# The linear half of the first expert bias: from TensorE to a row added by GpSimd

## The reference, cut to what matters

```python
def expert_block(args):
    xblk, e = args                                    # 128 tokens of expert e
    hh = xblk @ w1[e] + b1[e]                         # 1024 -> 2048, b1 is the "first bias"
    glu = jnp.minimum(hh[:, :D_FF], SWIGLU_LIMIT)     # first half of the 2048
    lin = jnp.clip(hh[:, D_FF:], -SWIGLU_LIMIT, SWIGLU_LIMIT)   # "linear" half
    act = glu * jax.nn.sigmoid(SWIGLU_ALPHA * glu) * (lin + 1.0)
    return act @ w2[e] + b2[e]
```

## Time and profile before

| | us | |
|---|---|---|
| median of three runs | 2273.63 | |
| profiled execution, whole | 2272.34 | |
| its span, first to last instruction | 2270.5 | 1.84 us lie around it |
| TensorE busy | 2235.7 | 98% |
| VectorE busy | 1768.0 | 78% |
| ScalarE busy | 1238.4 | 55% |
| GpSimd busy | 450.8 | 20% |

### The profile page before, as it was taken

The page is one execution under the profiler, slowest core; times in us unless marked ns, Lnnn a source line. Parts: engine busy times, 40 slices in busy tenths (PEclk is TensorE's granted clock), DMA queues, the critical chain, the costliest instruction groups (busy, mean ns, idle before and its releaser), DMA issues.

```text
span 2270.5 us, 30667 instructions
## 1 busy us (share of the span) xinstructions
PE 2235.7 (98%) x10681; PEld 1828.9 (81%) x10681; DVE 1768.0 (78%) x1652; ACT 1238.4 (55%) x1154; POOL 450.8 (20%) x422
## 2 busy tenths in 40 slices
PE   7999999999999999999999999999999999999997
PEld 3888888888887887888788888888888888888886
DVE  6756655555656766757899999999999999999996
ACT  6322132222225624632777777777777777777774
POOL 3000000000221131102522222232222222223222
PEclk9999999999999999999999999999999999999999
DMA  8322323131321121146899999999999999999995
GB/s 301 121 93 93 99 87 130 57 131 57 106 96 38 38 75 38 57 149 216 317 359 370 372 371 379 382 369 369 382 363 379 365 366 381 375 369 380 378 368 192
DMA packets 135517, 542.98 MB, mean 239 GB/s; under 512 B 16132, under 2 KB 24468, under 8 KB 101391
## 3 DMA queue, kind: packets, MB, share of 16 engines
q1 hardware_dynamic: 123192, 516.30, 60.2%
q0 software_dynamic: 11952, 21.44, 4.0%
q10 hardware_dynamic: 296, 4.21, 0.5%
HBM read 533.79 MB, written 26.38 MB: 247 GB/s over the span
## 4 chain that ended last, share of the span: by engine, by line
PE 95%; DMA 2%; DVE 1%; POOL 1%; issue 1%; ACT 0%; POOLq 0%; SPq 0%; DVEq 0%
PE ps L2263 90%; PE ps L2819 1%; PE ps L2831 1%; PE ps L2610 1%; DMA ar<-h_d,ar 1%; POOL list_d L865 1%; DMA ar<-in_ctx 0%; PE ps L2555 0%; DMA out_x<-ar,cur 0%; DMA raw<-in_w_mod 0%; PE ps L2501 0%; PE ps L2375 0%; DVE nmx L1866 0%; ACT hhi L1017 0%; PE ps L2708 0%
## 5 line engine op out<-in xcount | busy, mean ns | idle before, releaser
L2263 PE MATMUL ps<-whi,yhi 128*128 128x512 f32 x1072 | 346.4, 393 | 0.1
L2263 PE MATMUL ps<-hhi,yhi 128*128 128x512 f32 x1072 | 342.5, 389 | 0.0
L2083 DVE TENSOR_TENSOR hlo<-raw,hhi 128x2048 fp32r<-128x2048 f32 x132 | 302.7, 2294 | 47.2 <-ACT hhi L1324 47.2
L1324 ACT ACTIVATE whi<-raw 128x2048 fp32r<-128x2048 f32 x132 | 253.4, 1920 | 98.9 <-PE ps L2263 98.9
L2083 DVE TENSOR_TENSOR wlo<-raw,whi 128x2048 fp32r<-128x2048 f32 x132 | 298.8, 2284 | 3.3 <-ACT whi L1324 1.9
L1324 ACT ACTIVATE hhi<-raw 128x2048 fp32r<-128x2048 f32 x132 | 253.1, 1918 | 76.5 <-PE ps L2263 76.4
L1441 DVE TENSOR_TENSOR wlo<-raw,whi 128x2048 fp32r<-128x2048 f32 x56 | 128.2, 2289 | 159.4 <-ACT whi L986 159.4
L2263 PEld LDWEIGHTS ps<-whi,yhi 128*128 128x128 f32 x1072 | 201.2, 188 | 53.9 <-issue 12.1
L2263 PEld LDWEIGHTS ps<-hhi,yhi 128*128 128x128 f32 x1072 | 201.2, 188 | 41.8
L2263 PE MATMUL ps<-whi,hhi 128*128 128x512 f32 x592 | 233.3, 394 | 0.0
L2263 PE MATMUL ps<-whi,hlo 128*128 128x512 f32 x592 | 230.8, 390 | 0.0
(11 more groups left out here) (355 smaller groups left out, 4457.3 us busy)
## 6 DMA issues: line engine op xcount, KB each, us to landing
raw<-in_exp_w SPq DMA_DIRECT2D x264, 1024.0 KB, 8.3
ar<-in_exp_w SPq DMA_DIRECT2D x132, 1024.0 KB
raw<-in_w_in SPq DMA_DIRECT2D x44, 1024.0 KB, 5.1
raw<-in_w_mod SPq DMA_DIRECT2D x22, 1024.0 KB, 6.2
raw<-in_w_br_ret SPq DMA_DIRECT2D x8, 1024.0 KB, 5.3
ar<-in_x SPq DMA_DIRECT2D x8, 512.0 KB, 7.8
raw<-in_w_br_diff SPq DMA_DIRECT2D x4, 1024.0 KB, 5.2
raw<-in_w_out SPq DMA_DIRECT2D x4, 1024.0 KB, 10.7
```

Source lines behind the costliest of these rows:

```text
L1324: act.activation(e_whi[j % ESPL], e_raw[s], ACT.Copy).then_inc(e_hi, 1)
L2083: V.tensor_tensor(e_wlo[j % ESPL], e_raw[s], e_whi[j % ESPL].bitcast(F32), ALU.subtract).then_inc(e_lo, 1)
L2263: return pe.matmul(out, lhsT, rhs, start=start, stop=stop, skip_group_check=skip)
```

## The change

Banks 4 and 5 no longer get their bias from TensorE. `add_bias` keeps two matmuls (banks 2 and 3), and the first product of `up` now opens banks 4 and 5. The bias row of the linear half (with its 1) is stored once in a DRAM scratch by ScalarE's queue, and for every item SyncE's queue loads that item's row, broadcast to 128 partitions (512 KB), into `F(A_LIN)`. When `up(i)` is done, ScalarE copies banks 4 and 5 to `F(A_AC)` (`linear_out`), GpSimd adds the row in place (`add_linear_bias`, 128x1024), and VectorE clamps in place from SBUF and then multiplies. ScalarE's order becomes chunk 11, `linear_out`, `x_high`, `glu`; VectorE's becomes chunk 11, `x_low`, clamp, gate product. On GpSimd the addition stands between the selector and `next_gather`.

```diff
+            def load_linear_bias(e, i):
+                if not isinstance(i, int):
+                    sp.wait_ge(moe_step, i * 3)
+                sp.dma_start(F(A_LIN, D), acc_d[one(e), :].broadcast_to((P, D))).then_inc(b_loaded, 16)
...
+            sp.wait_ge(stored, 16 * (LT + 2))
+            load_linear_bias(0, 0)
             with sp.Fori(1, N_EXPERTS) as i:
                 for j in range(FIRST):
                     load_w1(i, i, j)
+                load_linear_bias(i, i)
                 for k in range(MOE_N - FIRST):
                     load_w2(i - 1, i, FIRST + k, k)
...
+            def add_linear_bias(i):
+                pool.wait_ge(b_loaded, i * 16 + 16 * (BIASES + 1))
+                pool.wait_ge(moe_step, i * 3 + 1)
+                hold()
+                pool.tensor_tensor(out=F(A_AC, D), in0=F(A_AC, D), in1=F(A_LIN, D), op=ALU.add).then_inc(moe_step, 1)
...
                 next_sel(i, e1)
+                add_linear_bias(i)
                 next_gather(i, code2, i * 4 + 1)
...
             next_sel(0, 1)
+            add_linear_bias(0)
             next_gather(0, 2, 1)
...
+            def linear_out(i):
+                act.wait_ge(e_used, chunk(i, FIRST - 1) + 1)
+                act.activation(F(A_AC, D), psf[:, 4 * COL:6 * COL], ACT.Copy).then_inc(moe_step, 1)
...
                 for j in range(ESPL, MOE_N - 1):
                     hi_e(i, j)
+                hi_e(i, MOE_N - 1)
+                linear_out(i)
+                x_high(i + 1)
                 glu(i)
-                hi_e(i, MOE_N - 1)
-                x_high(i + 1)
...
-            act.activation(bsrc[64:128, :], bsrc[64:128, :], ACT.Identity, bias=ones[64:128, 0:1]).then_inc(bias_hi, 1)
+            linear = F(A_LSRC, COL)[0:2 * N_EXPERTS, :]
+            act.activation(linear, linear, ACT.Identity, bias=ones[0:2 * N_EXPERTS, 0:1]).then_inc(bias_hi, 1)
+            act.activation(bias, F(A_BSRC, COL), ACT.Copy).then_inc(bias_hi, 1)
             act.wait_ge(bias_hi, 1)
-            for q in range(2):
-                act.activation(bias[q], bsrc[:, q * COL:(q + 1) * COL], ACT.Copy).then_inc(bias_hi, 1)
+            for r in range(2):
+                act.dma_start(acc_d[0:N_EXPERTS, r * COL:(r + 1) * COL],
+                              linear[32 * r:32 * r + 32, :]).then_inc(stored, 16)
...
-            def activate(i, between):
-
-                dve.wait_ge(e_used, chunk(i, FIRST - 1) + 1)
-                V.tensor_scalar(ac, psf[:, 4 * COL:6 * COL], 1.0 - LIMIT, 1.0 + LIMIT, ALU.max,
-                                ALU.min).then_inc(moe_step, 1)
-                between()
+            def activate(i):
+
+                dve.wait_ge(moe_step, i * 3 + 2)
+                V.tensor_scalar(ac, ac, 1.0 - LIMIT, 1.0 + LIMIT, ALU.max, ALU.min).then_inc(moe_step, 1)
                 dve.wait_ge(glu_done, i + 1)
-                dve.wait_ge(moe_step, i + 1)
+                dve.wait_ge(moe_step, i * 3 + 3)
...
-                activate(i, lambda: lo_e(i, MOE_N - 1))
+                lo_e(i, MOE_N - 1)
                 x_low(i + 1)
+                activate(i)
...
-                    for b in (0, 2, 1, 3):
-                        r = slice(b // 2 * 64, b // 2 * 64 + 64)
-                        last = mm(ps[:, 2 + b, :], sel[r, :], bias[b % 2][r], not late, False)
+                    for b in range(2):
+                        r = slice(b * 64, b * 64 + 64)
+                        last = mm(ps[:, 2 + b, :], sel[r, :], bias[r], not late, False)
...
-                        mm(o, xthi[:, kk, :], wh, late and kk == 0, False)
+                        mm(o, xthi[:, kk, :], wh, kk == 0 and (late or b > 1), False)
```

More of the change, by code:

```diff
@@ L137 @@
 A_XG, A_Y, A_GS, A_TH, A_AC = 0, 1024, 2048, 3072, 9216
+A_LIN, A_LSRC = A_TH, A_BSRC + COL
+BIASES = 6
 MOD_A = 2 * D // COL
@@ L474, in build @@
         hh = [h[:, :, :].rearrange("p a b -> p (a b)").rearrange("p (s k n) -> p s k n", s=3, k=KH) for h in (hhi, hlo)]
-        bias = [hh[0][:, 2, q, :] for q in range(2)]
+        bias = hh[0][:, 2, 0, :]
         sel = hh[0][:, 2, 2, 0:P]
@@ L696, in _ @@
             for r in range(4):
-                sp.dma_start(F(A_BSRC, D)[32 * r:32 * r + 32, :], a["exp_b1"][:, r // 2 * D:(r // 2 + 1) * D]).then_inc(b_loaded, 16)
+                sp.dma_start(F(A_BSRC, COL)[32 * r:32 * r + 32, :],
+                             a["exp_b1"][:, r // 2 * COL:(r // 2 + 1) * COL]).then_inc(b_loaded, 16)
+            for r in range(2):
+                sp.dma_start(F(A_LSRC, COL)[32 * r:32 * r + 32, :],
+                             a["exp_b1"][:, D + r * COL:D + (r + 1) * COL]).then_inc(b_loaded, 16)
             def one(e):
@@ L749, in extra @@
                     load_w1(e, i, j)
+                load_linear_bias(e, i)
                 for k in range(MOE_N - FIRST):
@@ L762, in _ @@
             sp.wait_ge(last_added, 32)
-            sp.wait_ge(stored, 16 * LT)
+            sp.wait_ge(stored, 16 * (LT + 2))
         @block.gpsimd
@@ L951, in _ @@
             next_sel(0, 1)
+            add_linear_bias(0)
             next_gather(0, 2, 1)
             pool.sem_inc(pool_m, 3)
-            pool.wait_ge(stored, 16 * LT)
+            pool.wait_ge(stored, 16 * (LT + 2))
             for t in range(LT):
@@ L1376, in _ @@
             hi_e(0, 1)
-            act.wait_ge(b_loaded, 64)
-            bsrc = F(A_BSRC, D)
-            act.activation(bsrc[64:128, :], bsrc[64:128, :], ACT.Identity, bias=ones[64:128, 0:1]).then_inc(bias_hi, 1)
+            act.wait_ge(b_loaded, 16 * BIASES)
+            linear = F(A_LSRC, COL)[0:2 * N_EXPERTS, :]
+            act.activation(linear, linear, ACT.Identity, bias=ones[0:2 * N_EXPERTS, 0:1]).then_inc(bias_hi, 1)
+            act.activation(bias, F(A_BSRC, COL), ACT.Copy).then_inc(bias_hi, 1)
             act.wait_ge(bias_hi, 1)
-            for q in range(2):
-                act.activation(bias[q], bsrc[:, q * COL:(q + 1) * COL], ACT.Copy).then_inc(bias_hi, 1)
+            for r in range(2):
+                act.dma_start(acc_d[0:N_EXPERTS, r * COL:(r + 1) * COL],
+                              linear[32 * r:32 * r + 32, :]).then_inc(stored, 16)
             hi_e(0, 2)
@@ L1394, in bias_out @@
                 if t == 0:
-                    act.wait_ge(stored, 16 * LT)
+                    act.wait_ge(stored, 16 * (LT + 2))
                 act.wait_ge(gb_done, t + 1)
@@ L1409, in _ @@
             act.activation(junk32[:, 0:1], ones[:, 0:1], ACT.Silu)
+            linear_out(0)
             glu(0)
@@ L2218, in _ @@
             dve.wait_ge(ones_made, 5)
[L2219 to L2223, removed]
+            dve.wait_ge(bias_hi, 2)
+            V.scalar_tensor_tensor(out=bias, in0=bias.bitcast(F32), scalar=low_rows[:, 0:1],
+                                   in1=F(A_BSRC, COL), op0=ALU.mult, op1=ALU.add).then_inc(bias_lo, 1)
             dve.wait_ge(gb_hi, 2)
@@ L2232, in _ @@
                 lo_e(1, j)
-            activate(0, lambda: None)
+            activate(0)
             x_low(1)
@@ L2852, in up @@
                         pe.wait_ge(xt_lo, 2)
-                        pe.wait_ge(bias_lo, 2)
+                        pe.wait_ge(bias_lo, 1)
                         add_bias()
```

## The result

The changed kernel takes **2289.97 us** in the median of four runs (2288.52 to 2292.82), the kernel before beside it 2272.93 (2272.01 to 2274.12): ratio 1.0076, 95% interval 1.0064 to 1.0088. It is slower by 17 us, where the prediction said 2274 (no change that one could measure) in a range of 2267 to 2291. The profiled execution has a span of 2291.0 us (2270.5 before), some 3 us above its own median, so the account of it that follows comes to more than 17.

What follows compares the result with a forecast made beforehand. The prediction took TensorE, busy 98% of the span, as the bound (loop period 35.30 us). Its terms -7.7 + 1.0 + 5.2 + 1.7 gave +0.2 us, so 2274 us, in a range of 2267 to 2291.

Steps and rivals of the forecast that it cites:

- main case: Whole kernel: all steps sum to +0.2 us, median 2274; 2268 to 2281 with its bounds; chance 0.42.
- rival (a): Expert loop: DMA becomes the bound, period 35.6 us at 381 GB/s, median 2291; chance 0.32.
- 2 and 3, gate path, VectorE: Looped items: the longer way to the gate product and VectorE's 33.8 of 35.06 us stay hidden, no stall.
- 5, half clock behind it: Behind the pause at the expert stage's start, TensorE's clock falls for 3.4 us: +1.7 us (0 to 3.4).
- Part 1: 32 looped items: one pair of bias matmuls less saves 0.24 us each, -7.7 us (to -10.9).
- rival (d): Bias matmuls: a lone pair takes as long as two, nothing saved, sum +7.9, 2281.5 us; chance 0.08.
- Part 2: Looped items, from `up` to `act_done`: addition 2.1 us, clamp 0.75, gate product ends at s + 8.7; no stall.
- Rival (b): GpSimd's addition is slow (longer than 3.2 us), so VectorE sets the period; 2307 us at 4.4; chance 0.05.
- Part 4: GpSimd's list in items 7, 14, 21, 28: addition 0 to 4 us late, 4 x 0.25 = +1.0 us (0 to 4).
- Part 6: One more 0.52 MB transfer for each item: landing hidden, the engines absorb it, zero cost.
- Part 5: Expert stage's start: first addition waits for the token lists, +5.2 us (3.9 to 6.5), and a clock fall, +1.7.
- Rival (c): Start costs 3.9 us without a clock fall and pairs save 0.34 each: -6.5 us, 2267; chance 0.13.

Runs made afterwards that it cites:

- experiment 2: Changed kernel with the bias scatter's landing awaited behind the copy for the next rows, in the four bias items: 2287.66 us, ratio 1.0063.
- experiment 3: Changed kernel without the 512 KB row transfer in each item (expert 0's row loaded once, used for all): 2288.23 us, ratio 1.0069.
- experiment 4: Changed kernel with both the earlier copy in the bias items and no row transfer for each item: 2273.83 us, ratio 1.0003.
- experiment 9: Kernel before, with two added 512 KB transfers in each item (14.1 MB for an item): 2310.6 us, ratio 1.0161.
- experiment 5: Changed kernel with GpSimd's first selector and first addition moved ahead of its wait for the token lists: 2286.51 us, ratio 1.0061.
- experiment 7: Changed kernel with 14 filler matmuls in place of 4 ahead of the first wait for the activation: 2289.73 us, against 2292.32 for the changed kernel beside it.
- (8): Kernel before, with one added 512 KB transfer in each item, never read: 2275.34 us, ratio 1.0008.
- (1): Changed kernel without the four scatters of bias rows in items 7, 14, 21 and 28: 2277.74 us, ratio 1.002.

## Why the prediction came out as it did

The main case failed: it added up to +0.2 us, and the measured change is +17. The time lies in the range, at its upper end, because the range was stretched to the 2291 of rival (a). That the two numbers meet is luck in good part: the rival had 31 periods of 35.6 us, and none of the plain items has that; the loss sits around four items, and GpSimd has its share in it. By the prediction's own parts, for the profiled pair:

| part | forecast | measured |
|---|---|---|
| 1, pairs | -7.7 | -7.3 |
| 2 and 3, gate path, VectorE | 0 | 0 where the loads are in time |
| 4, bias items | +1.0 (0 to 4) | +15.6, with 4.6 of it in two periods at a fallen clock |
| 5, start | +5.2 (3.9 to 6.5) | +6.3 |
| 5, half clock behind it | +1.7 | +1.9 (0.9 in the transposes, 1.0 in the first period) |
| 6, transfer | 0 | +2.5 in the tail, +1.5 in uneven periods, and part of the 15.6 |

**Part 1 held.** The full matmul follows the lone pair by 0.43 us:

```profile
1371.64 0.50 PE L2293 MATMUL ps<-hhi 64*128 64x512 f32 x2
1372.07 0.50 PE L2293 MATMUL ps<-whi,yhi 128*128 128x512 f32 x1
```

That ends rival (d).

**Part 2 held by its own steps.** The clamp from SBUF takes 0.69 us (0.75 forecast). The gate product ends at s + 8.5 (8.7). The addition's record is 3.52 us, but it begins 1.2 us before chunk 11's subtraction ends at 1363.34; where VectorE is idle it takes 2.34 (1118.84). `x_low`, with one SBUF input, ran beside it and cost nothing. Those are the two sides of the Trainium skill's rule on the port ("SBUF — State Buffer", Who interferes with whom), and the trace agrees. Rival (b) is out: VectorE is idle 1.1 us, against the 0.9 budgeted. What part 2 left out is the case of a late chunk 11: it took the start of `linear_out` from an item in which every load was in time, though its new order puts that copy behind the chunk, and with it a way to chunk 0 that is 1.9 us longer than before.

**Part 4 failed**, by its size. It let the addition come "0 to 4 us late", against some 2 us of room, and took 0.25 us for an item. No row gives that 0.25, and the bound of 4 us does not follow either: by its own far end four items lose 4 x (4 - 2) = 8 us. Item 8's addition ends at 1403.51 + 2.40 = 1405.91. In an ordinary item it ends 4.7 us behind the start of `linear_out` (1362.10 + 3.52 - 1360.92), here that is 1396.02 + 4.7 = 1400.7: so 5.2 us late, which less the 2 us of room is 3.2, and that item's period is 3.4 too long. So the price rule was right, and the lateness was taken from the cheap end of a range that was too short. The missing piece is the copy. The prediction took from the earlier trace rows that a GpSimd read gets in when a VectorE operation ends. From 1381.28 on the copy waited 6.38 us, past two ends of subtractions, until the third, behind which VectorE stood idle. Before, the copies in these four items met an operation with a PSUM input or the end of a row of subtractions, and took 0.18 to 0.29 us. What lets GpSimd in at one boundary and not at another is open. The half clock behind these stalls was not priced either, though the text priced it at the start. The third error is in kind: the part looked at GpSimd alone, as if each item had its own room. Experiments 2 to 4 show a second bound right behind.

**Part 6 failed.** "The engines absorb the transfer" was argued from the landing times of single loads. The rate was the better measure: by the earlier trace rows 388 GB/s were seen in one period and 387 were asked on average, and the text took the share of 1 as ambiguous. The rival's point of decision, 387 GB/s, was near the mark; the mean rate under too much demand is 389. The periods of 35.07 are there (so the rival's 35.6 is wrong), but a burst is not carried: by the estimate in experiment 9 each bias item leaves a debt that ordinary items pay back by 0.2 us each. That reading is argued from rates; what experiments 2 to 4 show is that the transfer costs 13.8 us once G is gone. How much of that is the rate and how much the longer way behind a late chunk is not parted. The Trainium skill's 358 GB/s was set aside for good reason, as 384 to 389 GB/s were held here.

**Part 5 held**, and the selector came at its far end, 1.3 us later than before. That may be scatter in part: in other traces with the transfer it came at 1117.15 to 1118.62, in two without it at 1116.08 and 1117.37. Experiments 5 and 7 confirm both terms, the pause and the clock; the clock was down for 6.8 us and not 3.4, at nearly the cost forecast. Rival (c), a cheap start, is out.

With both causes gone the kernel takes 2273.83 (experiment 4), near the predicted 2274, though not all for the same reasons: in its trace, the fastest of its ten runs, the start loses 4.0 us and not 7.2 (6.0 in experiment 3, also without the transfer).

## What to carry to other kernels

Before adding a transfer to a loop that runs at full DMA share, divide its bytes by the *new* period and compare with the rate that the loop holds over many periods (a few periods can do more, as the 399 GB/s of experiment 9 show); then do it again for the items with bursts, and ask how much each ordinary item can pay back. When an operation is put into a queue, walk through the worst item of that queue, not the ordinary one, with each landing and each blocked copy at its longest. When an order is changed, ask what now stands behind a load that can be late. And where an edit against one suspected cause gains little, take away both suspects before dropping either.

## What the runs showed of the hardware

- This stage gets 389 GB/s out of DMA over 31 periods (experiment 9), after 399 in the first seven; 384 were held with every period unchanged (8). Of the changed kernel, which asks for 387, 23 periods of 31 stood at 35.07 without the bias scatters (1), and 18 with them.
- Loads of 1 MB land after 8.3 us in one period of before; in the page of after the median is 10.2, in that of experiment 9 it is 12.4.
- A GpSimd copy of 128x2 stood 6.38 us behind back-to-back subtractions of VectorE with two SBUF inputs, until their row ended, though others got in between two of them (0.62 us in experiment 5).
- TensorE's clock was at 0.50 (1.2 GHz) behind a pause of 5.04 us, and stayed at 1.00 where the pause was 2.39 us or filled with matmuls (experiments 5 and 7). In the changed kernel two gaps of 2.12 and 1.03 us, with eight transposes between them, ahead of 1410.15 were enough: the window 1410.70 to 1414.00 has a clock of 0.50.
